# The second layer's head projections as matmuls over two halves of 256 columns

## The chip, the cores and the metric

One core of a Trainium2 chip runs the whole program. The metric is device time in microseconds (us); the time before is 1720.1 us, the median of two runs (1716.9 and 1723.3). Engines are called PE (TensorE matmuls), PEld (TensorE weight loads, which the profile lists beside the matmuls), DVE (VectorE), ACT (ScalarE), POOL (GpSimd) and SP (SyncE, which issues the weight transfers).

## What is computed

A decoder trunk of two layers over 512 tokens of width 1024, in float32, with inner width 2048 and 16 heads of 128. Each layer normalises, projects, mixes tokens, gates, projects back and adds to the residual. Layer 0 is a gated linear recurrence, layer 1 an attention in three dilated groups:

```python
for i in range(DEPTH):                       # 2
    u = rmsnorm(h, ln_g[i])
    y = hgrn2_mixer(u, ...) if i == 0 else dilated_attention_mixer(u, ...)
    h = h + y
return rmsnorm(h, final_g)

def dilated_attention_mixer(u, w_in, rel_bias, w_out):
    for g, (window, dilation) in enumerate(((128, 1), (512, 4), (2048, 16))):
        q = u @ w_in[:, 3*g*W : ...]          # each (512 x 1024) @ (1024 x 2048)
        k = ...; v = ...
        o, lse = dilated_group(q, k, v, table, window, dilation)
    o = sum over groups of softmax(lse) * o
    gate = u @ w_in[:, 9*W:]
    return (o * silu(gate)) @ w_out
```

In layer 1, three q, three k and one gate projection per head are the seven *head projections*: a 1024 x 128 slice of the weights against all 512 tokens.

## The kernel before

Everything contracts over 128 partitions at a time. The normalised activations `u` lie transposed in SBUF, as eight k-tiles of 128 features x 512 tokens. A float32 product is made of three matmuls on rounded operands (type fp32r): `u` and each weight tile `w` are split into a part `hi` and a rest `lo`, and hi x hi, hi x lo and lo x hi are summed in PSUM. In `split_matmuls` (L422) the three matmuls have a stationary operand of 128 x 128 and a moving operand of 512 columns. Every matmul brings a weight load of its own, also where the next one has the same stationary operand; in the profile the two are a row of PE and a row of PEld. The names of a PE row give the moving operand first: `proj<-u_lo,w_hi` streams `u_lo` against the stationary `w_hi`.

The program is written out in order, engine by engine, with semaphores. Heads go in four quads of four; three quads run in a hardware loop, the last is a second copy. In a quad of layer 1 (`at_body`) PE makes 7 head tiles for each head (`head_tile`), each in two halves of four k-tiles, 24 matmuls in all, that add up in one of three PSUM banks (`proj`). Behind each half it may do a piece of the attention of this or the head before: logits (L642, L654), transposes (L674), the sum over values (L686). These are plain float32, on 128 or 256 columns; the profile shows two PE and two PEld records for each such matmul (one for a transpose). Then come the value projections for the next quad (`values`: here `u` is stationary, for groups 1 and 2 with every fourth token, and `w` moves), and the out-projection (`out_column`). Layer 0 (`hg_body`) has three head tiles per head and the small matmuls of the recurrence (L565 to L597).

A head tile waits at its start for its weights (`w_ready`, counted up by DVE, which makes `w_lo` at L1023 from ACT's `w_hi` at L735) and for its bank (`bank_free`). Its last matmul raises `proj_done`, on which ACT waits to copy the bank to `qk` (L969), or to take the exponential of the gate. The weights arrive in four slots (`raw`) by transfers that SP issues when a slot's `w_lo` is done.

Of the kernel before, what the change touches and what calls it, by code (L numbers as in the profile page):

```python
# [36 lines left out]
P = 128  # L37
S = 512
D = 1024
W = 2048  # L40
KT = D // P
# [68 lines left out]
AT = Layer(HG.tiles, HG.events, 3 * NQ * HG.groups, 7, GROUPS)  # L110
# [15 lines left out]
def program(nc, x, ln_g, hg_w_in, hg_lb, hg_norm, hg_w_out, at_w_in, at_w_out, rel_bias, final_g,  # L126
            consts, onehot, relmask, out):
    ctx = ExitStack()
    with ctx:
        def sb(name, shape, dt=F32):  # L130
            return ctx.enter_context(nc.sbuf_tensor(name, shape, dt))
# [24 lines left out]
        u = {"hi": sb("u_hi", [P, KT, S], F32R), "lo": sb("u_lo", [P, KT, S], F32R)}  # L156
        hT = sb("hT", [P, KT, S])
        raw = sb("raw", [P, SLOTS, TW])
        w = {"hi": sb("w_hi", [P, SLOTS, TW], F32R), "lo": sb("w_lo", [P, SLOTS, TW], F32R)}
# [31 lines left out]
        cols = sb("cols", [P, 16])  # L191
# [13 lines left out]
        proj = [ctx.enter_context(nc.psum_tensor(f"proj{i}", [P, S], F32)) for i in range(BANKS)]  # L205
# [64 lines left out]
        def wait_emptied(eng, layer, q, e):  # L270

            _, bank, before = layer.event(q, e)
            eng.wait_ge(bank_free[bank], before + 1)
# [143 lines left out]
        def _(pe):  # L417
            def split_matmuls(bank, stationary, moving, first, last):

                ins = None  # L420
                for n, (a, b) in enumerate((("hi", "hi"), ("hi", "lo"), ("lo", "hi"))):
                    ins = nc.tensor.matmul(bank[:, :], stationary(a), moving(b),  # L422
                                           start=(first and n == 0), stop=(last and n == 2))
                return ins

            def head_tile(layer, q, n, half):

                number, slot, _ = layer.tile(q, n)
                _, bank, before = layer.event(q, n)
                if half == 0:  # L430
                    pe.wait_ge(w_ready, number + 1)
                    pe.wait_ge(bank_free[bank], before)
                for k in range(half * KT // 2, (half + 1) * KT // 2):
                    ins = split_matmuls(proj[bank], lambda a: w[a][:, slot, k * P:(k + 1) * P],
                                        lambda b: u[b][:, k, :], k == 0, k == KT - 1)
                if half:
                    ins.then_inc(proj_done, 1)

# [98 lines left out]
            for i in range(ST * KT):  # L537
                t, k = i // KT, i % KT
# [71 lines left out]
            def hg_body(q, last):  # L610
                for h in range(HQ):
                    for half in range(2 * HG.per_head):
                        head_tile(HG, q, HG.per_head * h + half // 2, half % 2)
                        if h:
                            recurrence(head(q, h - 1), h - 1, half)
                for half in range(KT):
                    if last:
                        out_column(HG, q, HG.heads + half // 2, HG.heads + half, half, range(HQ - 1))
                    else:
                        values(HG, q, 0, half // 2, half % 2)  # L620
                    recurrence(head(q, HQ - 1), HQ - 1, half)
                out_projection(HG, q, last)
# [76 lines left out]
            def at_body(q, last):  # L699
                for h in range(HQ):  # L700
                    for half in range(2 * AT.per_head):
                        head_tile(AT, q, AT.per_head * h + half // 2, half % 2)
                        if h:
                            attention(head(q, h - 1), h - 1, half - 1)
                        if half == 2 * K1:
                            natural_logits(q, h)
                        elif half == 2 * GA:
                            residue_logits(head(q, h), q, h)
                for half in range(KT if last else 2 * AT.pro):
                    if last:  # L710
                        out_column(AT, q, AT.heads + half // 2, AT.heads + half, half, range(HQ - 1))
                        attention(head(q, HQ - 1), HQ - 1, half - 1)
                    else:
                        if half == 2 * (ST - 1):

                            pe.wait_ge(res_logits, head(q, HQ - 1) + 1)
                        values(AT, q, half // 8, half // 2 % 4, half % 2)
                        attention(head(q, HQ - 1), HQ - 1, half - 1)
                out_projection(AT, q, last)
# [7 lines left out]
        def _(act):  # L727
# [9 lines left out]
            def copy_values(layer, q, group, e):  # L737
                _, bank, _ = layer.event(q, e)
                number = layer.event(q, e)[0]
                act.wait_ge(proj_done, number + 1)  # L740
                nc.scalar.activation(v_sb[group][:, (e - (0 if q is None else layer.heads)) % ST, :],  # L741
                                     value_bank(layer, q, e)[:, :], ACT.Copy).then_inc(bank_free[bank], 1)
# [273 lines left out]
        def _(dve):  # L1016
# [91 lines left out]
            def gate(layer, q, h, g, event):  # L1108

                _, bank, _ = layer.event(q, event)  # L1110
                dve.wait_ge(sigma_ready, g + 1)
                nc.vector.tensor_tensor(sg[:, :], proj[bank][:, :], eg[:, :], ALU.mult).then_inc(bank_free[bank], 1)  # L1112
# [343 lines left out]
```

## Time and profile before

| what | value |
|---|---|
| time, median of two runs | 1720.1 us (1716.9 to 1723.3) |
| profiled execution, from first to last instruction | 1719.9 us |
| PE | 1696.3 us busy, 99%, 8249 matmul records |
| PEld | 1446.8 us busy, 84%, 8249 records |
| DVE | 798.4 us busy, 46% |
| ACT | 642.7 us busy, 37% |
| transfers | 149.47 MB, mean 87 GB/s |
| layer 0 | about 0 to 606 us |
| layer 1 | about 606 to 1719.9 us |
| mean granted clock of PE, of full speed | 0.982 |

The profiled execution lies between the two timed runs; no other time of it is given than its span. The busy time of PE is that of records whose ends overlap the next record's start: a matmul of 512 columns is listed with 0.39 us, while the next one starts 0.23 us later. What a matmul occupies is therefore read from the starts of consecutive rows, or from a piece of the chain of waits (its length divided by its matmuls).

### The profile page before, as it was taken

To read this page: it belongs to the slowest core of one execution; us is meant where nothing else is said; L and a number is where in the kernel's file an instruction comes from. 1 tells how busy PE (TensorE), PEld (TensorE's weight loads), DVE (VectorE), ACT (ScalarE), POOL (GpSimd) and SP (SyncE) were. 2 spreads that over 40 slices of the span, in tenths; PEclk is the share of its full clock that TensorE was granted. 3 is DMA by queue.
4 is the path that set the end of the run, shared out by engine and by line. 5 is a ranking of instruction groups with operands and counts; after the bars stand their busy time and mean duration, and the time that the engine had idled before them with its cause. 6 is when DMAs were issued, how large, how long until landed. Compare 5 with 4: busy or idle time off the path is not lost.

```text
span 1719.9 us, 22142 instructions
## 1 busy us (share of the span) xinstructions
PE 1696.3 (99%) x8249; PEld 1446.8 (84%) x8249; DVE 798.4 (46%) x1363; ACT 642.7 (37%) x1088; POOL 20.8 (1%) x40
## 2 busy tenths in 40 slices
PE   7999999999999999999999999999999999999997
PEld 6888888888888689888899888889888889888886
DVE  6564574556465632444433344442344442334445
ACT  4443354343344333343332333333233333233333
POOL 0000000000000000000000000000000000000000
PEclk9999999998998999999999999999999999999999
DMA  6522321321321124433314323332333333333321
GB/s 208 158 69 73 92 64 45 110 73 61 91 69 61 39 85 117 98 81 84 89 54 122 98 62 87 91 86 91 113 93 80 93 68 98 98 93 82 87 54 62
DMA packets 247998, 149.47 MB, mean 87 GB/s; under 512 B 47040, under 2 KB 227648, under 8 KB 247920
## 3 DMA queue, kind: packets, MB, share of 16 engines
q1 hardware_dynamic: 203328, 139.69, 29.4%
q0 software_dynamic: 2608, 8.39, 1.5%
q10 hardware_dynamic: 41984, 0.27, 1.3%
q8 instruction: 59, 0.97, 0.2%
q14 instruction: 19, 0.16, 0.0%
HBM read 146.02 MB, written 6.50 MB: 89 GB/s over the span
## 4 chain that ended last, share of the span: by engine, by line
PE 97%; DVE 1%; ACT 1%; issue 0%; DMA 0%; SPq 0%; DVEq 0%; ACTq 0%
PE proj L422 80%; PE inner L565 4%; PE inner L686 3%; PE inner L654 2%; PE inner L422 2%; PE inner L674 2%; PE inner L642 1%; PE inner L587 1%; PE inner L590 1%; PE inner L576 1%; PE inner L569 0%; DMA v<-x 0%; DVE v L1405 0%; PE inner L544 0%; PE inner L531 0%
## 5 line engine op out<-in xcount | busy, mean ns | idle before, releaser
L1023 DVE TENSOR_TENSOR w_lo<-raw,w_hi 128x1024 fp32r<-128x1024 f32 x252 | 308.0, 1223 | 483.2 <-ACT w_hi L735 482.1
L422 PE MATMUL proj<-u_hi,w_hi 128*128 128x512 f32 x1280 | 514.6, 402 | 0.0
L422 PE MATMUL proj<-u_hi,w_lo 128*128 128x512 f32 x1280 | 503.1, 393 | 0.0
L422 PE MATMUL proj<-u_lo,w_hi 128*128 128x512 f32 x1280 | 503.0, 393 | 0.0
L735 ACT ACTIVATE w_hi<-raw 128x1024 fp32r<-128x1024 f32 x252 | 265.3, 1053 | 133.6 <-PE proj L422 118.5
L422 PEld LDWEIGHTS proj<-u_hi,w_lo 128*128 128x128 f32 x1280 | 243.1, 190 | 52.7
L422 PEld LDWEIGHTS proj<-u_lo,w_hi 128*128 128x128 f32 x1280 | 243.7, 190 | 48.7
L422 PEld LDWEIGHTS proj<-u_hi,w_hi 128*128 128x128 f32 x1280 | 243.4, 190 | 48.8 <-issue 0.3
L422 PE MATMUL proj<-w_hi,u_hi 128*128 128x512 f32 x472 | 191.8, 406 | 6.7 <-issue 3.7
L422 PE MATMUL proj<-w_lo,u_hi 128*128 128x512 f32 x472 | 189.2, 401 | 0.0
L422 PE MATMUL proj<-w_hi,u_lo 128*128 128x512 f32 x472 | 188.9, 400 | 0.0
L422 PEld LDWEIGHTS proj<-w_hi,u_hi 128*128 128x128 f32 x472 | 121.8, 258 | 18.9 <-issue 8.9
L422 PEld LDWEIGHTS proj<-w_hi,u_lo 128*128 128x128 f32 x472 | 121.8, 258 | 9.4
L422 PEld LDWEIGHTS proj<-w_lo,u_hi 128*128 128x128 f32 x472 | 122.1, 259 | 8.5
L969 ACT ACTIVATE qk<-proj 128x512 f32<-128x512 f32 x96 | 57.0, 594 | 161.7 <-PE proj L422 161.7
L899 ACT ACTIVATE rows<-rows,negm 128x256 f32<-128x256 f32 (+1 forms) x128 | 61.9, 484 | 140.8 <-DVE negm L1303 135.6
L422 PE MATMUL proj<-y_hi,w_hi 128*128 128x512 f32 x256 | 103.4, 404 | 0.9 <-DVE sg L1112 0.7
L422 PE MATMUL proj<-y_lo,w_hi 128*128 128x512 f32 x256 | 100.2, 391 | 0.0
L422 PE MATMUL proj<-y_hi,w_lo 128*128 128x512 f32 x256 | 100.1, 391 | 0.0
L741 ACT ACTIVATE v<-proj 128x512 f32<-128x512 f32 x59 | 35.1, 596 | 138.8 <-PE proj L422 127.2
L1205 DVE TENSOR_TENSOR hT<-hT,proj 128x512 f32<-128x512 f32 x80 | 54.4, 686 | 69.0 <-PE proj L422 68.7
L565 PEld LDWEIGHTS inner<-rows,keys 128*32 128x32 f32 (+3 forms) x512 | 53.6, 156 | 13.1 <-issue 5.3
(156 smaller groups left out, 1497.0 us busy)
## 6 DMA issues: line engine op xcount, KB each, us to landing
raw<-at_w_in SPq DMA_DIRECT2D x160, 512.0 KB, 4.1
raw<-hg_w_in SPq DMA_DIRECT2D x64, 512.0 KB, 4.2
raw<-hg_w_out SPq DMA_DIRECT2D x16, 512.0 KB, 3.6
raw<-at_w_out SPq DMA_DIRECT2D x16, 512.0 KB, 4.4
v<-x SPq DMA_DIRECT2D x4, 512.0 KB, 6.5
bias_tiles<-ext_rows POOLq DMA_DIRECT2D x1, 2048.0 KB, 11.8
bias_tiles<-ext_rows POOLq DMA_DIRECT2D x2, 1024.0 KB, 17.6
bias_n<-bias_tiles POOLq DMA_DIRECT2D x16, 128.0 KB, 4.1
```

Source lines behind the costliest of these rows:

```text
L422: ins = nc.tensor.matmul(bank[:, :], stationary(a), moving(b), start=(first and n == 0), stop=(last and n == 2))
L565: ins = nc.tensor.matmul(p_sc[0:seen, b * P + j * CH:b * P + (j + 1) * CH], keys[:, b, j, 0:seen], qd[:, b * P + j * CH:b * P + (j + 1) * ...
L576: ins = nc.tensor.matmul(p_U[:, b * P:(b + 1) * P], kT[:, b, :], v_sb[0][:, b, h * P:(h + 1) * P], start=True, stop=True)
L654: ins = nc.tensor.matmul(p_S[r // 2][:, ((r % 2) * 2 + i) * P:((r % 2) * 2 + i + 1) * P], qk[:, 2 + 2 * i, s], qk[:, 3 + 2 * i, s], start= ...
L674: ins = nc.tensor.transpose(p_T[n % 2][:, (i % 4) * P:(i % 4 + 1) * P], src, ident[:, :])
L686: ins = nc.tensor.matmul(o, vals, pT[:, i, :], start=(i == 0), stop=(i == len(TILES) - 1), skip_group_check=True)
L735: nc.scalar.activation(w["hi"][:, slot, :], raw[:, slot, :], ACT.Copy).then_inc(hi_ready, 1)
L741: nc.scalar.activation(v_sb[group][:, (e - (0 if q is None else layer.heads)) % ST, :], value_bank(layer, q, e)[:, :], ACT.Copy).then_inc( ...
L899: nc.scalar.activation(probs[:, i, 0:n], probs[:, i, 0:n], ACT.Exp, bias=negm[:, i:i + 1], accum_out=stat[:, i // ST, 1, b:b + 1]).then_in ...
L969: nc.scalar.activation(o, src, ACT.Copy, scale=QSCALE if i in (Q0, Q1, Q2) else 1.0)\
L1023: nc.vector.tensor_tensor(w["lo"][:, slot, :], raw[:, slot, :], w["hi"][:, slot, :].bitcast(F32), ALU.subtract).then_inc(w_ready, 1)
L1205: nc.vector.tensor_tensor(hT[:, k, :], hT[:, k, :], proj[bank][:, :], ALU.add)\
```

## The change

In layer 1, `head_tile` calls a new helper, `half_matmuls`, in place of `split_matmuls`. It goes over the 512 tokens in two halves `t`; for each it issues the three matmuls with the moving operand cut to 256 columns and the output to the same 256 columns of the bank. The bank is cleared for accumulation by the first matmul of the tile alone. Layer 0, the values, the out-projections and the attention are as they were.

```diff
+            def half_matmuls(bank, stationary, moving, first, last):
+
+                for t in range(2):
+                    cols = slice(t * (S // 2), (t + 1) * (S // 2))
+                    for n, (a, b) in enumerate((("hi", "hi"), ("hi", "lo"), ("lo", "hi"))):
+                        ins = nc.tensor.matmul(bank[:, cols], stationary(a), moving(b)[:, cols],
+                                               start=(first and t == 0 and n == 0), stop=(last and n == 2),
+                                               skip_group_check=True)
+                return ins
+
             def head_tile(layer, q, n, half):
...
                 for k in range(half * KT // 2, (half + 1) * KT // 2):
-                    ins = split_matmuls(proj[bank], lambda a: w[a][:, slot, k * P:(k + 1) * P],
-                                        lambda b: u[b][:, k, :], k == 0, k == KT - 1)
+                    several = half_matmuls if layer is AT else split_matmuls
+                    ins = several(proj[bank], lambda a: w[a][:, slot, k * P:(k + 1) * P],
+                                  lambda b: u[b][:, k, :], k == 0, k == KT - 1)
```

PE at the end of the first half of head tile K1 in layer 1, where the natural logits follow; before:

```order
L422 MATMUL proj2<-u_hi,w_hi 128x512
L422 MATMUL proj2<-u_lo,w_hi 128x512
L422 MATMUL proj2<-u_hi,w_lo 128x512
L273 REGISTER_ALU
L642 MATMUL inner0<-qk 128x128
```

And now:

```order
L431 MATMUL proj2<-u_hi,w_hi 128x256
L431 MATMUL proj2<-u_lo,w_hi 128x256
L431 MATMUL proj2<-u_hi,w_lo 128x256
L431 MATMUL proj2<-u_hi,w_hi 128x256
L431 MATMUL proj2<-u_lo,w_hi 128x256
L431 MATMUL proj2<-u_hi,w_lo 128x256
L273 REGISTER_ALU
L653 MATMUL inner0<-qk 128x128
```

The last k-tile of the half has six matmuls in place of three; the wait and the logits stand behind them as before. All other engines have the same instructions in the same order. Each matmul of a head projection in layer 1 now appears twice, with its weight load.

## Rows read from the trace of the kernel before

**Rows 1.** The page: span, and busy time of each engine (share) xinstructions.

```profile
span 1719.9 us, 22142 instructions
PE 1696.3 (99%) x8249; PEld 1446.8 (84%) x8249; DVE 798.4 (46%) x1363; ACT 642.7 (37%) x1088; POOL 20.8 (1%) x40
```

**Rows 2.** The page, chain of waits: shares of the span by engine and line.

```profile
PE 97%; DVE 1%; ACT 1%; issue 0%; DMA 0%; SPq 0%; DVEq 0%; ACTq 0%
```

**Rows 3.** Waits of PE, ACT and DVE: us in total, times, longest.

```profile
PE inner L544 <- DMA ident<-consts: 4.7, 1, 4.7
PE proj L422 <- issue: 3.7, 1, 3.7
PE proj L422 <- DVE u_lo L1043: 3.0, 1, 3.0
...
ACT qk L969 <- PE proj L422: 161.7, 56, 4.6
...
DVE w_lo L1023 <- ACT w_hi L735: 482.1, 189, 16.7
```

**Rows 4.** Groups by form, 606 to 1720 us: xcount | busy us, mean ns.

```profile
L422 PE MATMUL proj<-u_hi,w_hi 128*128 128x512 f32 x896 | 356.0, 397 | 0.0
L422 PE MATMUL proj<-u_hi,w_lo 128*128 128x512 f32 x896 | 349.4, 390 | 0.0
L422 PE MATMUL proj<-u_lo,w_hi 128*128 128x512 f32 x896 | 348.7, 389 | 0.0
```

**Rows 5.** Timeline of a head tile: start us, duration us, engine, line.

```profile
1000.12 0.39 PE L422 MATMUL proj<-u_lo,w_hi 128*128 128x512 f32 x1
1000.12 0.19 PEld L422 LDWEIGHTS proj<-u_hi,w_lo 128*128 128x128 f32 x1
...
1001.48 0.39 PE L422 MATMUL proj<-u_lo,w_hi 128*128 128x512 f32 x1
1001.48 0.19 PEld L422 LDWEIGHTS proj<-u_hi,w_lo 128*128 128x128 f32 x1
```

**Rows 6.** Chain of waits, pieces in order of time: start us, us, what, xmatmuls.

```profile
1002.10 0.87 PE inner L674 x8
...
1009.24 3.35 PE inner L686 x30
1012.59 1.52 PE inner L642 x8
```

**Rows 7.** Timeline of the values with every fourth token stationary.

```profile
914.76 0.40 PE L422 MATMUL proj<-w_lo,u_hi 128*128 128x512 f32 x1
914.76 0.31 PEld L422 LDWEIGHTS proj<-w_hi,u_lo 128*128 128x128 f32 x1
...
917.81 0.40 PE L422 MATMUL proj<-w_hi,u_lo 128*128 128x512 f32 x1
```

**Rows 8.** Timeline of layer 0's first values.

```profile
20.70 0.63 PE L422 MATMUL proj<-w_hi,u_hi 128*128 128x512 f32 x1
...
21.98 0.63 PE L422 MATMUL inner<-w_hi,u_hi 128*128 128x512 f32 x1
```

**Rows 9.** Stretches: from:to us, busy us of PE PEld DVE ACT POOL, PEclk, DMA, GB/s.

```profile
18.60:22.80 4.20, 4.20 (x11) 3.27 (x10) 4.16 (x7) 2.43 (x5) 0.00 (x0) 0.50 0.51 101
562.70:566.10 3.40, 3.40 (x31) 2.95 (x32) 3.08 (x4) 1.35 (x2) 0.00 (x0) 0.99 0.18 24
566.20:569.40 3.20, 3.20 (x11) 2.72 (x12) 1.97 (x6) 0.49 (x1) 0.00 (x0) 0.50 0.80 261
617.50:1719.00 1101.50, 1092.70 (x5305) 950.30 (x5303) 439.03 (x732) 379.47 (x706) 16.08 (x30) 1.00 0.34 87
```

**Rows 10.** Timeline behind the residue logits: head matmuls.

```profile
710.51 0.40 PE L422 MATMUL proj<-u_lo,w_hi 128*128 128x512 f32 x1
710.75 0.40 PE L422 MATMUL proj<-u_hi,w_lo 128*128 128x512 f32 x1
710.98 0.40 PE L422 MATMUL proj<-u_hi,w_hi 128*128 128x512 f32 x1
711.22 0.39 PE L422 MATMUL proj<-u_lo,w_hi 128*128 128x512 f32 x1
```

## The prediction

> **What bounds the kernel now.** I read the page first. PE is busy for 99% of the span, with 8249 matmuls and as many weight loads [rows 1], and the chain of waits is PE for 97% [rows 2]. So time can go or come only where PE's own stream gets shorter or longer. The waits say the same: PE's three longest are one each of 4.7, 3.7 and 3.0 us, all at the start or between the layers, while ACT waits 161.7 us for the head projections and DVE 482.1 us for ACT's halves of the weights, which come once a slot is free [rows 3]. The other engines follow PE; none is near its limit. What the change touches are the three groups of the head projections in layer 1, 896 matmuls each, 2688 together [rows 4]. The question is then only how long one of them holds PE, and how long two halves of it would.
>
> A group's mean duration (389 to 397 ns) doesn't tell this, since records overlap. The timeline does: from 1000.12 to 1001.48 us there are six starts, 1.36 / 6 = 226.7 ns from one matmul to the next [rows 5]. At the full clock of 2.4 GHz (PEclk 1.00 in all of layer 1 [rows 9]) 512 columns at one a cycle are 213.3 ns. The matmul holds PE for 13.4 ns more than its columns. Its weight load starts with the matmul before (both at 1000.12) and is listed with 0.19 us: it is hidden.
>
> **The change, step by step.** Removed: 2688 matmuls of 512 columns, 2688 x 226.7 ns = 609.4 us of PE. Added: 5376 matmuls of 256 columns with 5376 weight loads. The columns are as many as before. So everything hangs on two prices: what of the 13.4 ns is paid per matmul and what per column, and how short the interval can get before the weight load no longer hides.
>
> *The weight load.* The trace shows short matmuls in plain float32. 30 of 128 columns take 3.35 us, 111.7 ns each, and the natural logits 1.52 us for 8, of which two have 128 columns: (1.52 - 0.22) / 6 = 217 ns for one of 256 [rows 6]. That fits two cycles a column (106.7 and 213.3 ns) and a few ns on top, so each streams for as long as a half of ours (256 columns at one cycle, 106.7 ns) or twice that. With 106.7 ns of streaming and a load of 128 columns for each, 111.7 ns is the interval: load and stream run side by side. How long a load really holds its path I take from a place where it is the bound. With every fourth token as stationary operand the load is listed with 0.31 us instead of 0.19, and 13 intervals from 914.76 to 917.81 give 234.6 ns [rows 7]: the listed time less 75 ns. The same subtraction makes 115 ns of 0.19, close to the 111.7 ns of the 128-column matmuls. So I take it that a load alone sets a floor of about 112 ns, the same for both types. Two halves can't be done in less than 2 x 111.7 = 223.4 ns: the lower bound is a gain of 3.3 ns a pair, 2688 x 3.3 = 9 us, or 1711 us.
>
> *The overhead.* At 256 columns the load's floor of 111.7 ns lies close to the stream's 106.7, so the 13.4 ns decide. No row has an fp32r matmul of another width than 512. Between ends:
> - all per column: a half is 226.7 / 2 = 113.4 ns, just above the load's floor; change 0;
> - all per matmul: 106.7 + 13.4 = 120.1 ns; a pair 240.1 ns, plus 13.4 ns, 2688 x 13.4 = **36.0 us**.
>
> I take the second. In plain float32 the part on top of the columns is small at each width (5 ns at 128 columns, 3 to 4 at 256 [rows 6]); it does not grow with them, so what this engine adds is added per instruction there. The half-speed rows say that the extra isn't cycles of the array: from 20.70 to 21.98 us, three intervals at granted clock 0.50 are 1.28 / 3 = 427 ns, and 512 columns at 1.2 GHz are 426.7 [rows 8, 9]. At half speed the 13.4 ns are gone, hidden behind the slower stream. A step ahead of the array that costs some fixed time at each matmul would look like this, but so would a feed that delivers fp32r columns a little slower than one in 0.417 ns; that is why the other end keeps a good part of the chance. The intervals behind a stretch of plain float32 speak for the fixed one: from 710.51 to 710.75, 710.98 and 711.22 they are 230 to 240 ns, and return to 227 later, with the same 512 columns [rows 10]. What lies on top of the columns moves with what stands around the matmul, not with its columns.
>
> *The rest.* The waits of a head tile stand where they stood, once in 24 matmuls before and in 48 now; they are met early. The copies out of a bank are as many and as large, and ACT, which waits for PE there, has more time. Weight transfers and `w_lo` stay the same and are asked for later. PE gets twice the instructions; at 120 ns it takes them no faster than the 30 matmuls at 111.7 ns [rows 6], though those are a burst and a half tile now has 24 and more in a row. All of this I cost at nothing. Sum: 1719.9 + 36.0 = 1755.9 us for the profiled execution, which lies 0.2 us below the median, so **1756 us**, 2.1% more.
>
> *What a page would say.* The row shows 226.7 ns for 512 columns [rows 5]. The Trainium skill, "TensorE: Matmul & The Clock Gate", section "Back-to-back issue gap", gives a warm matmul N / 2.4 + 2.5 ns, and under "LDWEIGHTS (loading the stationary operand)" columns / 1.2 for a load, 107 ns here. By that an estimate for a half is 109 ns, and the change costs 2688 x 2.5 = 7 us instead of 36. For 512 columns it makes 216 ns, which this trace contradicts by 11 ns; its load agrees with the 112 ns floor.
>
> **The rivals.**
> 1. *Little or nothing: the extra goes by column* (not slower). If fp32r columns are fed at 226.7 / 512 = 0.443 ns each, a half takes 113.4 ns and the time is 1720 us. If some 3 ns of it are per matmul, as in the float32 rows [rows 6], and only the rest by column, a pair costs 3 ns more and the time is 1728 us; If load and stream both settle at their floor it is 1711 us. It decides as long as a half takes under about 118.5 ns: 2688 x 12.8 ns is 34.4 us, 2% of the time. For it: the extra at the full clock, none at half. Against: the constant part in the float32 rows. The Trainium skill's rule above gives a time of this rival's kind. Chance 0.24: 0.22 between 1715 and 1735, 0.02 below.
> 2. *Load and stream disturb each other more.* Now the load takes about half of the matmul's time; at 256 columns they run side by side all the time, and stay as they are behind a float32 stretch. There the interval is up to 237 ns, 23 over the columns [rows 10]. With that in each half, a pair is 2 x 130 = 260 ns, plus 33: 2688 x 33 = 89 us, 1809 us; half of the way is 1782 us. Against: 30 matmuls at 111.7 ns run with both side by side and show no such thing, in the other type. Chance 0.12.
> 3. *A half costs as much as a whole*, because the fp32r load isn't hidden in so short a stream, or fp32r falls to the two cycles a column of plain float32 (217 ns). Then 2688 x (2 x 217 to 227 - 226.7) = 557 to 611 us: 2277 to 2331 us. Against: loads are listed alike for both types, and their bound in [rows 7] fits. Chance 0.06.
> 4. *The clock falls.* In layer 0 it was at 0.50 right behind a stretch of recurrence matmuls of 32 columns, with PE listed as busy throughout [rows 9]. If gaps between halves counted like that, such a stretch of 3.2 us at half clock costs 1.6 us; one for each of the 16 heads makes 26 us on top, 1782 us. Against: the columns still fill 107 of 120 ns. Chance 0.03.
>
> The forecast has 0.55. It lies hardly above 2% (34.4 us), about what a measurement of this kernel can tell from no change, so I split it: 0.36 of it over, 0.19 within. Faster by over 2% nothing in the rows allows; 0.01. Slower: 0.36 + 0.12 + 0.06 + 0.03 = 0.57 and within: 0.19 + 0.23 = 0.42. The range takes in the forecast, nearly all of rival 1 and the lower half of rival 2: **1715 to 1790 us**. The likeliest case alone is 1750 to 1764.
>
> **What would show it.** In the changed kernel's timeline two starts in a head tile of layer 1 lie 120 ns apart if I am right, 113 for rival 1, 130 for rival 2, over 200 for rival 3. The three groups have 1792 matmuls each and PEld shows 10937 records, where all are recorded. Layer 0's end stays at about 606 us, the values and out-projections keep their 227 and 235 ns, PEclk stays at 1.00 in layer 1. ACT's wait for the head projections grows by a part of the 36 us. I am wrong if the interval isn't 120 ns, or if PE shows idle time that it didn't have.

## The result, and the profile after

The changed kernel takes 1761.7 us (1761.3 to 1762.1, 2 runs) against 1720.1 us: 1.0232 times the time before, 95% interval 1.0184 to 1.028. In more rounds (the run `again` below) the ratio is 1.0208 (1.0189 to 1.0227). It is slower, by about 2%, and whether by more or less than 2% the intervals leave open; the forecast was 1756 us. The profiled execution took 1762.1 us, of which 1760.3 are its span.

The page of the changed kernel, as in [rows 1] and [rows 2]:

```profile
span 1760.3 us, 27518 instructions
...
PE 1737.2 (99%) x10937; PEld 1593.7 (91%) x10937; DVE 797.4 (45%) x1363; ACT 642.5 (37%) x1088; POOL 20.8 (1%) x40
...
PE 97%; DVE 1%; ACT 1%; DMA 0%; issue 0%; SPq 0%; DVEq 0%; ACTq 0%
```

There are 2688 more matmuls and weight loads, nothing else is added, and PE is as much the bound as it was. The timeline inside a head tile of layer 1 answers to [rows 5]:

```profile
1000.05 0.28 PE L431 MATMUL proj<-u_hi,w_hi 128*128 128x256 f32 x1
1000.05 0.19 PEld L431 LDWEIGHTS proj<-u_lo,w_hi 128*128 128x128 f32 x1
...
1001.25 0.28 PE L431 MATMUL proj<-u_lo,w_hi 128*128 128x256 f32 x1
1001.25 0.19 PEld L431 LDWEIGHTS proj<-u_hi,w_lo 128*128 128x128 f32 x1
```

Ten intervals, 1.20 us: 120 ns for a half. Over all 5256 intervals between neighbouring head-projection matmuls of layer 1 (those that begin at the first or the last of an unbroken sequence left out) the trace has 119.9 ns on average. The listed duration fell only from 0.39 to 0.28 us, so a reader of mean durations would have seen 283 x 2 = 566 ns against 390 and taken the change to cost far more than it does.

Where did the 40.4 us between the spans (1760.3 - 1719.9) go? The chain of waits has the first value matmuls of layer 1 here, before the change and after it (start us, us, what):

```profile
602.98 3.65 PE proj L422 x9
```

```profile
610.06 3.72 PE proj L422 x9
```

So 7.1 us of the 40.4 came in layer 0, which wasn't changed, and 33.3 in layer 1. The granted clock explains the first part. These are the stretches from 0 to 603 us before and from 0 to 610 us after (from:to us, busy us of PE PEld DVE ACT POOL, PEclk, DMA share, GB/s):

```profile
0.00:603.00 603.00, 589.10 (x2890) 484.65 (x2890) 346.79 (x616) 255.85 (x373) 4.75 (x10) 0.95 0.30 87
```

```profile
0.00:610.00 610.00, 596.53 (x2889) 490.05 (x2889) 346.54 (x616) 255.77 (x373) 4.74 (x10) 0.94 0.29 86
```

The clock records have 54.6 us at one half in layer 0 before, and 71.7 after; half of the difference, 8.5 us, is what that costs at most. In layer 1 the clock stays full from 617.5 us on, as in [rows 9]. Each of the two traces also has 3.4 us at half clock within a microsecond of layer 1's first value matmul, ahead of these windows (at 603.6 us before, 610.6 after):

```profile
617.50:1757.00 1139.50, 1133.18 (x8024) 1097.65 (x8022) 442.92 (x739) 382.69 (x711) 16.07 (x30) 1.00 0.33 84
```

The followers wait longer for PE (waits: us in total, times, longest), and PE's own longest waits are those of [rows 3]. ACT's wait at its copy to `qk` grows from 161.7 to 186.7 us; for two of the 68 times, 8.4 us, the profile names no releaser:

```profile
DVE w_lo L1034 <- ACT w_hi L746: 507.9, 189, 16.7
ACT qk L980 <- PE proj L431: 178.3, 66, 5.0
...
ACT qk L980 <- issue: 8.4, 2, 4.2
...
PE inner L555 <- DMA ident<-consts: 4.7, 1, 4.7
PE proj L422 <- issue: 3.7, 1, 3.7
PE proj L422 <- DVE u_lo L1054: 3.0, 1, 3.0
```

### The profile page after: what moved, and what is told of

It is laid out like the page before. It is cut to its first block, busy times and chain, and to the rows that moved or that the text cites. A ratio compares the mean times of both kernels' runs of the same rounds, so it can differ in the third digit from the quotient of the medians.

```text
span 1760.3 us, 27518 instructions
## 1 busy us (share of the span) xinstructions
PE 1737.2 (99%) x10937; PEld 1593.7 (91%) x10937; DVE 797.4 (45%) x1363; ACT 642.5 (37%) x1088; POOL 20.8 (1%) x40
## 4 chain that ended last, share of the span: by engine, by line
PE 97%; DVE 1%; ACT 1%; DMA 0%; issue 0%; SPq 0%; DVEq 0%; ACTq 0%
PE proj L422 44%; PE proj L431 36%; PE inner L576 4%; PE inner L697 3%; PE inner L665 2%; PE inner L422 2%; PE inner L685 2%; PE inner L653 1%; PE inner L598 1%; PE inner L601 1%; PE inner L587 1%; PE inner L580 1%; DMA v<-x 0%; DVE v L1416 0%; PE inner L542 0%
## 5 line engine op out<-in xcount | busy, mean ns | idle before, releaser
L431 PE MATMUL proj<-u_hi,w_hi 128*128 128x256 f32 x1792 | 513.8, 287 | 0.1
L431 PE MATMUL proj<-u_hi,w_lo 128*128 128x256 f32 x1792 | 507.8, 283 | 0.0
L431 PE MATMUL proj<-u_lo,w_hi 128*128 128x256 f32 x1792 | 507.6, 283 | 0.0
L431 PEld LDWEIGHTS proj<-u_hi,w_hi 128*128 128x128 f32 x1792 | 344.1, 192 | 1.0 <-issue 0.5
L431 PEld LDWEIGHTS proj<-u_lo,w_hi 128*128 128x128 f32 x1792 | 344.1, 192 | 0.5
L431 PEld LDWEIGHTS proj<-u_hi,w_lo 128*128 128x128 f32 x1792 | 343.9, 192 | 0.0
L746 ACT ACTIVATE w_hi<-raw 128x1024 fp32r<-128x1024 f32 x252 | 265.1, 1052 | 132.7 <-PE proj L422 118.5
L422 PE MATMUL proj<-u_hi,w_hi 128*128 128x512 f32 x384 | 162.2, 422 | 0.0
L422 PE MATMUL proj<-u_lo,w_hi 128*128 128x512 f32 x384 | 157.6, 410 | 0.0
L422 PE MATMUL proj<-u_hi,w_lo 128*128 128x512 f32 x384 | 156.6, 408 | 0.0
L980 ACT ACTIVATE qk<-proj 128x512 f32<-128x512 f32 x96 | 57.0, 594 | 186.7 <-PE proj L431 178.3
```

What stands on the lines that cost most here:

```text
L431: ins = nc.tensor.matmul(bank[:, cols], stationary(a), moving(b)[:, cols], start=(first and t == 0 and n == 0), stop=(last and n == 2), sk ...
L746: nc.scalar.activation(w["hi"][:, slot, :], raw[:, slot, :], ACT.Copy).then_inc(hi_ready, 1)
L980: nc.scalar.activation(o, src, ACT.Copy, scale=QSCALE if i in (Q0, Q1, Q2) else 1.0)\
```

## The experiments

Times are against the kernel before on the same chip. "Layer 1" is the time from its first value matmul to the last transpose of PE in the profiled execution: 1108.3 us before, 1141.6 after the change.

**again.** The changed kernel as it is.

> The changed kernel itself, timed in more rounds. The theory: the change costs 13.4 ns for each of the 2688 pairs of halves, 36 us, and the further 4.4 us between the two spans come from how often layer 0 fell to half clock in the one profiled execution of each. Then over more rounds the ratio is 1.0210 (1756 against 1720), and layer 0 is as long in both on average. The rival: the change also costs something outside the head tiles of layer 1 (twice the instructions to fetch, say); then the ratio stays at 1.0235 or so, with layer 0 or the values longer.

Measured: 1759.4 us, ratio 1.0208 (1.0189 to 1.0227), the forecast's 2.1%. Layer 1 took 1142.0 us, again 33.7 more than before, with layer 0 ending at 606.2 us and 64.9 us of it at half clock. So the change costs 33 to 34 us in layer 1, and what is above that comes and goes with layer 0's clock.

**alternate.** The two loops of the helper changed places.

```diff
-                for t in range(2):
-                    for n, (a, b) in enumerate(...):
+                for n, (a, b) in enumerate(...):
+                    for t in range(2):
```

> The halves in the other order: for each of the three products both halves of the tokens, so that four of six neighbours share the stationary operand and no two neighbours write the same columns of the bank. The theory (a fixed 13.4 ns for each matmul, whatever its neighbours): 120 ns from start to start, 1.00 against the changed kernel, about 1756 to 1762 us. The rival that a matmul waits for the sum of the one before it in the same columns, or that a repeated stationary operand is cheaper: 107 to 113 ns, 1720 us or less.

Measured: ratio 1.0179 (1.0159 to 1.0199); layer 1 1141.4 us, the interval 119.9 ns. A row merges two neighbours with the same operands:

```profile
999.93 0.40 PE L431 MATMUL proj<-u_hi,w_hi 128*128 128x256 f32 x2
1000.17 0.40 PE L431 MATMUL proj<-u_lo,w_hi 128*128 128x256 f32 x2
1000.41 0.40 PE L431 MATMUL proj<-u_hi,w_lo 128*128 128x256 f32 x2
```

0.24 us for each two. Neither the columns that the neighbour wrote nor a repeated stationary operand makes a difference to the interval: the rival falls. That the 13.4 ns are fixed for each matmul, the first theory, isn't shown by this; the narrow operands below speak against it.

**quarters** and **uneven.** The columns cut at 128, 256 and 384, or at 320.

```diff
-                for t in range(2):
-                    cols = slice(t * (S // 2), (t + 1) * (S // 2))
+                for t in range(4):
+                    cols = slice((0, 128, 256, 384, 512)[t], (0, 128, 256, 384, 512)[t + 1])
```

> Layer 1's head projections in four operands of 128 columns. The theory (stream plus 13.4 ns, but never under the floor of a load of 128 columns, 112 ns): 4 x 111.7 = 447 ns for what were 226.7, 2688 x 220 = 592 us, about 2312 us. Without that floor 4 x 66.7 = 267 ns, 107 us more, 1827 us. If fp32r fell to a slower rate in so short an operand, four cycles a column, 213 ns and more each: 4 x 216 = 864 ns, about 3433 us.

Measured: 2310.0 us, ratio 1.3438 (1.3355 to 1.3521), two microseconds from the expectation. The interval is 111.7 ns, eight of them in 0.89 us:

```profile
1000.17 0.28 PE L431 MATMUL proj<-u_lo,w_hi 128*128 128x128 f32 x1
...
1001.06 0.28 PE L431 MATMUL proj<-u_hi,w_hi 128*128 128x128 f32 x1
```

At one column a cycle the stream would take 53 ns, so something else sets this. The load of 128 columns is the reading that fits: the float32 matmuls of [rows 6] have the same 111.7 ns, and with the longer loads of [rows 7] the interval grew. It is argued, not shown, since no run has 128 moving columns with a shorter load; two cycles a column would give nearly the same time at 128 columns, and only the next run speaks against that, for 192.

> Layer 1's head projections in operands of 320 and 192 columns, so that as many matmuls are made as with halves. Stream plus 13.4 ns with a floor of 112 ns for the load: 146.7 and 111.7 (its stream would be 93.4), 258.4 ns a pair, 31.7 over the whole operand, 2688 x 31.7 = 85 us, about 1805 us. If the extra were a fixed time for each matmul and the load no bound: 240.1 ns, as with halves, 1756 to 1762 us. If an operand under 256 columns is streamed slower, at four cycles a column: 146.7 + 323, over 2300 us.

Measured: 1802.8 us, ratio 1.0488 (1.0427 to 1.0548). As many matmuls as with halves, and 41 us more: a pair takes 257.6 ns (expected 258.4). That is the sum of 146.7 ns for 320 columns with the same 13.4 ns on top, and of the floor for 192; at two cycles a column 192 columns alone would take 160 ns. Only the sum fits, though: from the first 192 of a k-tile on, the six intervals are on average 88, 113, 113, 169, 146 and 147 ns, so some 23 ns move from the first 192 to the first 320. Why isn't shown. Two k-tiles, six pairs in 1.55 us:

```profile
1000.01 0.25 PE L431 MATMUL proj<-u_hi,w_hi 128*128 128x192 f32 x1
...
1001.56 0.25 PE L431 MATMUL proj<-u_hi,w_hi 128*128 128x192 f32 x1
```

**narrow, narrow64, narrow_whole.** Fewer columns of the stationary operand, so a shorter load; the last with 512 moving columns. Each also writes to fewer partitions of the bank, which no run separates from the shorter load.

```diff
-                    ins = several(proj[bank], lambda a: w[a][:, slot, k * P:(k + 1) * P],
+                    wide = P // 4 if layer is AT else P         # P // 2 in narrow64
+                    ins = several(proj[bank][0:wide, :], lambda a: w[a][:, slot, k * P:k * P + wide],
```

> As the changed kernel, but the stationary operand of layer 1's head projections is cut to 32 of its 128 columns, so that the load is a quarter as long; the other 96 outputs of each tile are left out. Three causes of the 120 ns. (1) The extra belongs to the matmul: 106.7 + 13.4 = 120 ns as before, 1756 to 1762 us. (2) The load is the bound, its 107 ns and a change-over of 13.4: then the stream is the bound, 107 to 110 ns, 5376 x 10 to 13 ns = 54 to 70 us less than the changed kernel, about 1697 us. (3) The load takes cycles from the stream as it reads: a quarter of 13.4 ns is left, 110 ns, about 1705 us.

Measured: ratio 1.0021 (1.0008 to 1.0034), the profiled execution 1717.4 us; layer 1 1110.3 us, 31 less than in the changed kernel. The weight load is listed with 0.11 us in place of 0.19, and five intervals take 0.57 us, 114 ns each (114.3 on average over layer 1, and 113.3 where they have settled), not 120 and not 110:

```profile
999.78 0.28 PE L431 MATMUL proj<-u_hi,w_hi 128*32 128x256 f32 x1
999.90 0.28 PE L431 MATMUL proj<-u_lo,w_hi 128*32 128x256 f32 x1
1000.01 0.28 PE L431 MATMUL proj<-u_hi,w_lo 128*32 128x256 f32 x1
...
1000.35 0.28 PE L431 MATMUL proj<-u_hi,w_lo 128*32 128x256 f32 x1
```

None of the three causes is right as written. The extra isn't the matmul's alone (1), since it halves from 13.3 to 6.7 ns; the load isn't simply the bound (2), since a quarter of the load doesn't free all of it; and it isn't in proportion (3).

> As the run with 32 columns of the stationary operand, with 64 of its 128 (the other 64 outputs of each tile are left out). With 128 columns a half took 119.9 ns, with 32 113.3 to 114.3: if the extra is a constant and a part for each column loaded (0.06 to 0.07 ns), the interval is 115.5 to 116.2 ns. If instead the load's end is what the next matmul waits for beyond some length, 64 columns give the same as 32, 113 to 114 ns.

Measured (one profiled execution, 1723.7 us): 113.3 ns where they have settled and 114.2 on average, the same as with 32. A constant with a slope is out; half of the stationary columns left out already gives the full relief.

```profile
999.82 0.28 PE L431 MATMUL proj<-u_hi,w_hi 128*64 128x256 f32 x1
...
1001.07 0.28 PE L431 MATMUL proj<-u_hi,w_lo 128*64 128x256 f32 x1
```

Eleven intervals in 1.25 us.

> The kernel before the change (512 columns), with the stationary operand of layer 1's head projections cut to 32 of 128 columns (the other 96 outputs of each tile are left out). If the extra is a constant and a part for each column loaded, and does not depend on how long the stream is: 213.3 + 6.6 = 220 ns. If the stream of 512 has an extra of its own by column: 223 ns or more.

Measured (one profiled execution, 1737.5 us): layer 1 1119.3 us, 11 more than before the change. Nearly all intervals are 229 to 235 ns, 231.4 on average against 227.4: with the *shorter* load the 512 columns were slower.

```profile
999.72 0.39 PE L422 MATMUL proj<-u_lo,w_hi 128*32 128x512 f32 x1
...
1002.50 0.39 PE L422 MATMUL proj<-u_lo,w_hi 128*32 128x512 f32 x1
```

Twelve intervals in 2.78 us, 232 ns. The alternative of the expectation (223 ns or more) came true, but not for its reason, since 256 columns with the same load have an extra of 6.7 and 512 one of 18 ns: that is neither by column nor by matmul.

**bf16_whole** and **bf16_halves.** Constant bfloat16 tiles as operands of layer 1's head projections.

```diff
+                    st = (lambda a: bf_w[:, :]) if layer is AT else ...    # 128 x 128
+                    mv = (lambda b: bf_u[:, :]) if layer is AT else ...    # 128 x 512
```

> Layer 1's head projections with operands of 512 columns as before the change, but on constant bfloat16 tiles in place of the fp32r activations and weights (their content is left out of the computation; waits, banks and number of matmuls are the same). If the 13.4 ns belong to the type (four bytes a column read at full clock): 216 ns from start to start, the few ns of the plain float32 rows on top of 213.3, 2688 x 11 = 29 us less than the kernel before, about 1691 us. If they belong to any matmul with its load: 226.7 ns and 1720 us.

> The same constant bfloat16 tiles in two halves of 256 columns. If the type makes the extra: 109 to 112 ns each (106.7 and 3, or the load's floor of 112 unless a bfloat16 load is shorter), 1693 to 1705 us, so a split costs 2 to 14 us. If the extra is that of any matmul: 120 ns, 1756 us.

Measured: 1693.7 us, ratio 0.9853 (0.9794 to 0.9912), and 1700.8 us, ratio 0.9879 (0.9859 to 0.9898). Whole:

```profile
999.76 1.67 PE L427 MATMUL proj<-bf_u,bf_w 128*128 128x512 bf16 x7
```

and halves:

```profile
1000.18 1.15 PE L436 MATMUL proj<-bf_u,bf_w 128*128 128x256 bf16 x9
```

(1.67 - 0.38) / 6 = 215 ns and (1.15 - 0.28) / 8 = 109 ns; over all neighbours 215.8 and 109.2. Here there are 2.5 ns on top of each stream at both lengths, and layer 1 grows by 7.0 us from whole to halves (1079.4 to 1086.5), 2.6 ns a pair. So 11 of the 13.4 ns are gone with these tiles. The type is the likely reason, but not the only difference: the tiles are constant and always the same two, and their load is listed with 0.10 us in place of 0.19. The shorter load alone doesn't do it, since fp32r with a load of 0.11 us has 18 ns at 512 columns and 6.7 at 256; constant fp32r tiles were not run.

**both_layers.** `several = half_matmuls` in layer 0 too.

> The halves in layer 0's head tiles too: 1152 more pairs. The theory: 13.4 ns each, 15.5 us at full clock, nothing of it while the clock is at one half (427 ns for 512 columns, so 213 for 256); layer 0 runs at half clock for some 10% of its time, so about 14 us more than the changed kernel, 1771 us against 1757 (ratio to the kernel before 1.029 to 1.030). The rival that the extra depends on what stands around in layer 1 (attention, transfers): 0 or over 25 us more. If more weight loads made the clock fall more often, over 30 us more.

Measured: ratio 1.0164 (1.0143 to 1.0184): not 14 us more than the changed kernel but 7 less. The clock is what I had not reckoned with: it fell less often, and not more often as the last rival had it. Layer 0 in this run, 599.4 us in place of 603 to 610:

```profile
0.00:599.40 599.40, 586.40 (x4041) 534.65 (x4042) 347.68 (x616) 255.32 (x373) 4.76 (x10) 0.98 0.30 88
```

21.9 us of it are at half clock instead of 55 to 72, which saves some 16 to 25 us and hides the cost of the halves. Where the clock is at half, a half operand takes about 213 ns, half of the 427 in [rows 8], so there a split is free; five intervals in 1.06 us:

```profile
67.84 0.42 PE L431 MATMUL proj<-u_hi,w_lo 128*128 128x256 f32 x1
...
68.90 0.41 PE L431 MATMUL proj<-u_lo,w_hi 128*128 128x256 f32 x1
```

The question was then what lets it fall. Before the change there are 11 pieces at half clock inside layer 0, apart from its start and end, and each begins in the last 1.1 us of a stretch of score matmuls of 32 columns or up to 0.5 us behind it. Such a stretch stands in each of the 16 heads, so 5 have none. The first (chain of waits, then the stretches):

```profile
63.86 3.67 PE inner L565 x32
67.53 0.43 PE inner L569 x3
67.96 4.26 PE proj L422 x12
```

```profile
63.60:67.50 3.90, 3.90 (x35) 3.27 (x34) 1.22 (x2) 0.79 (x2) 0.00 (x0) 1.00 0.75 213
67.70:71.10 3.40, 3.40 (x10) 2.73 (x9) 0.74 (x4) 0.49 (x1) 0.00 (x0) 0.50 0.16 48
```

PE is listed as busy in both.

**split_scores** and **split_scores_both.** The scores in two parts, in the kernel before and with halves in both layers.

```diff
-            def scores(g):
+            def scores(g, part):
-                pe.wait_ge(keys_ready, g + 1)
-                for b in range(ST):
+                if part == 0:
+                    pe.wait_ge(keys_ready, g + 1)
+                for b in (2 * part, 2 * part + 1):
...
                 if half == 0:
-                    scores(g)
+                    scores(g, 0)          # and the transposes of the keys
                 elif half == 1:
+                    scores(g, 1)
                     updates(g, h)
```

> The kernel before, with one other change: in layer 0 the 16 score matmuls of a head (32 records of 32 columns, 3.9 us in one piece) stand in two parts, the second behind the next half of a head tile. In the runs so far layer 0 had 27 to 72 us at half clock, every piece but the first and last right behind such a stretch, and not behind each of them. The theory: it is these stretches that let the clock fall, and layer 0's length differs between runs by how many do. Then only the pieces at the start and between the layers stay, some 10 us at half clock, and the time is 20 to 27 us under the kernel before, 1693 to 1700 us, with less scatter between runs. The rival: the clock falls by the mean over a longer time, or at any float32 work; then it falls as often and the time is 1720 us or a little more. If the later scores hold up DVE and ACT, PE gets waits in layer 0.

Measured: 1699.4 us, ratio 0.9863 (0.9844 to 0.9882), 24 us less, and four runs within 1.8 us of each other where nine of the kernel before lie within 7.8. The clock of layer 0, and its scores now:

```profile
63.80 1.84 PE inner L566 x16
65.64 0.36 PE inner L572 x3
66.00 2.75 PE proj L422 x12
```

```profile
0.00:582.00 582.00, 568.72 (x2889) 464.83 (x2890) 344.91 (x616) 254.65 (x373) 4.75 (x10) 0.99 0.31 90
```

6.8 us at half clock are left, all at the start; layer 0 ends at 582.0 us, 21 earlier, and layer 1 takes the same 1108.4. The theory holds so far: with the stretches in two parts the clock never fell inside layer 0 beyond its start. What decides behind which of the whole stretches it falls stays open: both_layers has the same 16, and it fell at 3. This version is the fastest, 1.4% under the kernel before.

> The same split of the scores with the halves of 256 columns in both layers. The theory: at an undisturbed clock the halves cost 12.4 ns a pair in layer 1 (2688 pairs, 33.4 us) and 12 to 13.4 ns in layer 0 (1152 pairs, 14 to 15 us), 48 us over the kernel with split scores alone; layer 0 of the run with halves in both layers was short only because its clock fell at 3 of the stretches instead of 11 to 14. The rival that the halves in layer 0 cost nothing or help there: 33 us or less.

Measured: 1750.0 us, ratio 1.0163 (1.0144 to 1.0182), 50.7 us over split_scores (48 expected). In layer 0 it is 10.6 us, or 12.3 when 3.4 us less at half clock are allowed for: 10.7 ns for each of the 1152 pairs, where 12 to 13.4 were expected. So the halves do cost something in layer 0, and the rival falls; why it is 1 to 3 ns a pair less than expected stays open. Layer 1 is 38.5 us longer, 5 more than the halves cost alone. That is a new wait at the turn of the quad loop, which neither kernel has:

```profile
944.96 1.48 PE proj L431 x11
946.44 1.72 issue
948.17 3.93 PE proj L431 x19
```

It comes twice, 3.5 us in all, with 3.4 us at half clock behind the first, which costs at most 1.7 us more and makes up the 5 us with them; both_layers has it too (2.8 us).

## Why the prediction was right

**What bounds the kernel.** Right. PE is 97% of the chain before and after, and its own waits are unchanged.

**The price of a half.** Predicted 120.1 ns, measured 119.9. The choice between "by column" (113) and "by matmul" (120) was the whole forecast, and it fell rightly for these shapes: the order of the halves didn't matter, the sum of the uneven pair fits 13.4 ns at 320 columns too, and in layer 0 an extra of 10.7 ns a pair came again.

**The reason given for it** holds only in part. I argued from the constant few ns of the float32 rows that what PE adds is added per instruction. One of these rows can't carry that: the 5 ns at 128 columns are the same 111.7 ns that I had just taken for the load's floor, so they say nothing on the stream. The bfloat16 runs show a part per matmul, 2.5 ns. The other 11 ns of fp32r are not a fixed time for a matmul: with 32 stationary columns 6.7 ns stay at 256 moving columns and 18 at 512. The numbers of stationary and of moving columns both count. What in the hardware makes it was not settled; no run here separates further. With 128 stationary columns the extra happens to be about 13.3 ns at both widths that I compared, and so the sum came out: the number is right by a reason that is only half right, and that part is luck.

**The floor**, 112 ns, drawn from the strided loads and the float32 rows, was right as a number: quarters have 111.7. That it is the load's is the reading that fits all rows, not one that a run isolates.

**The sum.** 36.0 us were predicted, 33.3 and 33.7 measured in layer 1. The term removed was a little small: I took 226.7 ns for each, but behind each stretch of float32 matmuls some ten have 224 to 237 ns [rows 10], and their mean over all head tiles of layer 1 is 227.4. The halves aren't longer there: after the first, those behind such a stretch average 117 to 122 ns and settle at 120 after six. 2688 x (2 x 119.9 - 227.4) = 33.3 us. The other 7.1 us between the two profiled executions lie in layer 0's clock, which the prediction had as unchanged ("layer 0's end stays at about 606 us"; it was 603.0 before the change already, and 610.1 after). In more rounds most of that evens out: the medians of `again` lie 35.1 us apart. So the forecast's 36 meets the measured time a little better than the 33 to 34 us that the halves cost, which is chance. The last step also compared a span with timed runs, which are 1.9 us longer than their spans here (1762.1 and 1760.3); that is too little to matter.

**What was costed at nothing** was nothing: waits, copies, transfers, since the pairs alone account for layer 1. Twice the instructions cost nothing in this kernel; where layer 0 had them too, a wait came at the turn of layer 1's loop, with a cause that wasn't tested.

**The rivals.** Rival 1 would have needed 113 ns, rival 2 some 130, rival 3 over 200: the interval excludes them. The border given for rival 1 was reckoned wrongly: 12.8 ns more on a pair of 226.7 is 119.7 ns for a half, not 118.5, so the forecast's 120.1 lay hardly above it. Rival 2's evidence, the longer intervals behind a float32 stretch, doesn't carry over to halves at all. Rival 4, the clock in layer 1, did not come: PEclk is 1.00 from 617.5 us on. The clock mattered, but in layer 0 and in both kernels. On the rule weighed in the prediction: the Trainium skill, "TensorE: Matmul & The Clock Gate", section "Back-to-back issue gap", gives N / 2.4 + 2.5 ns as the gap of a single warm matmul. The bfloat16 intervals, 215.8 and 109.2 ns, agree with it within 0.1 ns, and the fp32r intervals, 227.4 and 119.9, lie 11 to 12 ns above it.

## What to carry to other kernels

Read a matmul's price from the starts of consecutive rows, and before cutting its moving operand ask what stands on top of its columns and how short an interval its weight load allows: each part pays the former again, and a part whose columns take less than the latter, 112 ns here in fp32r with 128 stationary columns, gives nothing back. If PE is busy throughout, look at the granted clock by stretches as well: a few microseconds of short matmuls in one piece, repeated in each head, can cost nearly as much as the edit under study, and putting longer matmuls between them got 24 us back here, where the edit cost 33 to 34. When two profiled executions are compared, take the changed part from its own start to its own end, so that what varies elsewhere stays out.

## What was not expected of the hardware

- An fp32r matmul of 256 columns takes 113.3 ns with 32 or 64 stationary columns and 119.9 with 128, but one of 512 columns takes 229 to 235 with 32 and 226.7 with 128 (settled intervals).
- The granted clock fell to one half at 11 to 14 of layer 0's 16 stretches of score matmuls (before the change, after it, and in `again` and `alternate`) with PE listed as busy, at 9 in `narrow` and at 3 in `both_layers`; with the stretches in two parts of 1.8 us it never did.
- At the turn of the quad loop PE stood for 1.4 to 1.8 us without anything that it waited for, only in the two kernels with halves in both layers. Instruction transfers had grown from 59 packets to 104 (80 with halves in layer 1 alone, and no such wait). But `quarters` has 121 packets, more matmuls in that loop than any other run, and no such wait either, so the number alone doesn't make it. Whether the fetching of instructions is the cause was not tested.
